# Two buffers of a tuned fp32 kernel start 16 bytes past a multiple of 64

## What is computed

```
h = rms_norm(x); proj = h @ w_in            # retention heads and latent attention, then @ w_out
x = x + conv_ffn(rms_norm(x), w_up, conv_w, conv_b, w_down)
... second block, twice:
  y = mixer(modulate(x)) ; x = layer_norm(alpha*x + g1*y)
  f = peer(modulate(x))  ; x = layer_norm(alpha*x + g2*f)

peer:  s = top-k of query @ keys             # 16 experts for each of 8 heads and each token
       act  = gelu(sum_d h * u_tab[idx])
       out  = sum_k (gate * act) * v_tab[idx]
```

## Time and profile before

| | |
|---|---|
| median of three runs | 2287.6 us (2285.16 to 2290.14) |
| profiled execution | 2285.66 us, of which the span from the first to the last instruction is 2284.3 us |
| mean granted TensorE clock | 0.993 of full speed |
| busy: PE, PEld, DVE, ACT, POOL | 98%, 83%, 82%, 53%, 7% of the span |
| moved by DMA | 442 MB, 194 GB/s over the span |

### The profile page before, as it was taken

The page is one execution under the profiler, slowest core; times in us unless marked ns, Lnnn a source line. Parts: engine busy times, 40 slices in busy tenths (PEclk is TensorE's granted clock), DMA queues, the critical chain, the costliest instruction groups (busy, mean ns, idle before and its releaser), DMA issues.

```text
span 2284.3 us, 34778 instructions
## 1 busy us (share of the span) xinstructions
PE 2233.5 (98%) x13446; PEld 1889.3 (83%) x13446; DVE 1864.8 (82%) x3365; ACT 1201.4 (53%) x1754; POOL 168.5 (7%) x75
## 2 busy tenths in 40 slices
PE   9999999999999999999999999999999999999997
PEld 7789978777788888888887877788888888888886
DVE  8679996568689988888888888869998888887656
ACT  7555554466456555554444445455665554444553
POOL 0000000000044400000000000014430000000000
PEclk9999999999999999999999999999999999999999
DMA  8366593233556655555558996455655555556664
GB/s 292 125 203 217 196 355 117 93 120 102 184 176 185 191 177 170 172 174 175 171 176 306 340 352 233 148 185 186 189 187 169 175 172 171 175 175 223 219 234 136
DMA packets 123508, 442.32 MB, mean 194 GB/s; under 512 B 13760, under 2 KB 16832, under 8 KB 122704
## 3 DMA queue, kind: packets, MB, share of 16 engines
q1 hardware_dynamic: 117464, 425.04, 56.3%
q10 hardware_dynamic: 5880, 15.06, 1.9%
HBM read 436.88 MB, written 3.16 MB: 193 GB/s over the span
## 4 chain that ended last, share of the span: by engine, by line
PE 82%; DVE 10%; ACT 3%; DMA 3%; issue 2%; SPq 0%; ACTq 0%; DVEq 0%
PE psum L447 21%; PE psum L457 13%; PE psum L459 13%; PE psum L458 13%; PE psum L451 12%; PE psum L452 3%; PE psum L2863 3%; DVE low L2607 3%; DVE acc L1784 2%; DMA ring<-in_peer_v 2%; DVE cv L2115 1%; ACT spl L1104 1%; ACT cv L1405 1%; PE psum L925 1%; PE psum L2806 1%
## 5 line engine op out<-in xcount | busy, mean ns | idle before, releaser
L2607 DVE TENSOR_TENSOR low<-ring,spl 128x1024 fp32r<-128x1024 f32 x638 | 778.7, 1228 | 259.3 <-ACT spl L1104 258.8
L1104 ACT ACTIVATE spl<-ring 128x1024 fp32r<-128x1024 f32 x702 | 735.2, 1054 | 281.7 <-DMA ring<-in_peer_u 155.3
L447 PE MATMUL psum<-hT,spl 128*128 128x512 f32 x2016 | 520.0, 397 | 2.5 <-ACT yy_abo L1454 1.4
L447 PEld LDWEIGHTS psum<-hT,spl 128*128 128x128 f32 x2016 | 375.5, 189 | 76.7 <-DVE hT L2454 3.6
L457 PE MATMUL psum<-spl,Ws 128*128 128x512 f32 x1024 | 407.1, 398 | 6.9 <-DVE Ws L2645 6.8
L459 PE MATMUL psum<-spl,Ws 128*128 128x512 f32 x1024 | 399.5, 390 | 0.0
L458 PE MATMUL psum<-low,Ws 128*128 128x512 f32 x1024 | 398.4, 389 | 0.0
L451 PEld LDWEIGHTS psum<-hT,low 128*128 128x128 f32 x2304 | 315.7, 191 | 22.6
L451 PE MATMUL psum<-hT,low 128*128 128x256 f32 x2304 | 322.5, 283 | 0.0
L1713 ACT ACTIVATE Ws<-S 128x256 fp32r<-128x256 f32 x256 | 106.6, 417 | 354.5 <-PE psum L459 349.8
L2920 POOL TENSOR_TENSOR low<-ring,spl 128x1024 fp32r<-128x1024 f32 x64 | 162.1, 2534 | 1133.5 <-ACT spl L1104 1133.5
(11 more groups left out here) (411 smaller groups left out, 2900.1 us busy)
## 6 DMA issues: line engine op xcount, KB each, us to landing
ring<-in_peer_u SPq DMA_DIRECT2D x256, 512.0 KB, 3.5
ring<-in_peer_v SPq DMA_DIRECT2D x256, 512.0 KB, 3.6
vring<-in_ada_w SPq DMA_DIRECT2D x56, 512.0 KB, 6.1
ring<-in_w_up SPq DMA_DIRECT2D x44, 512.0 KB, 5.0
aring<-in_ada_w SPq DMA_DIRECT2D x40, 512.0 KB, 4.9
ring<-in_ab_in SPq DMA_DIRECT2D x32, 512.0 KB, 3.5
ring<-in_peer_wq SPq DMA_DIRECT2D x32, 512.0 KB, 3.8
ring<-in_w_down SPq DMA_DIRECT2D x22, 512.0 KB, 5.9
```

The costliest lines, as they stand in the source:

```text
L447: q.matmul(wide, w(hi, k), P.hT[:, :, k, :], start=k == 0, stop=False)
L1104: q.activation(P.spl[:, m % SLOTS, 0:w], P.ring[:, m % SLOTS, 0:w], ACT.Copy).then_inc(*P.hi.mark(m))
L2607: q.tensor_tensor(P.low[:, n % SLOTS, 0:w], P.ring[:, n % SLOTS, 0:w], P.spl[:, n % SLOTS, 0:w].bitcast(F32), ALU.subtract).then_inc(*P.lo ...
```

## The change

The buffers `ring` and `spl` are allocated 32 words (128 bytes) longer, and their five tiles are taken from word 4 on, so that each tile starts 16 bytes past a multiple of 64. `low` keeps the address of `ring`. All buffers behind the two move up: `spl` by 128 + 16 bytes, everything from `hT` on by 256 bytes, which leaves them as they were modulo 64 and modulo 256. Tile shapes, instructions, waits and their order stay the same.

```diff
         low = self.base + 4 * self.at_word
-        self.ring = f("ring", [128, SLOTS, 1024])
-        self.low = nc.alloc_sbuf_tensor_at("low", [128, SLOTS, 1024], F32R, offset=low)
-        self.spl = f("spl", [128, SLOTS, 1024], F32R)
+        tiles = lambda t: t[:, 4:4 + SLOTS * 1024].rearrange("p (s w) -> p s w", s=SLOTS)
+        self.ring = tiles(f("ring", [128, SLOTS * 1024 + 32]))
+        self.low = tiles(nc.alloc_sbuf_tensor_at("low", [128, SLOTS * 1024 + 32], F32R, offset=low))
+        self.spl = tiles(f("spl", [128, SLOTS * 1024 + 32], F32R))
         self.hT = f("hT", [128, 2, 8, 256], F32R)
```

## The result

The changed kernel took 2296.94 us (median of six runs, 2295.19 to 2301.47) beside 2287.45 us of the kernel before (six runs, 2285.16 to 2290.58): a ratio of 1.0044, 95% interval 1.0033 to 1.0054, or 9.5 us. Forecast were 2287.5 us and a range up to 2300 with "same" as likeliest; by the bound of 0.2% it is slower. The change to the time is clear of the noise, and the forecast of its direction was wrong.

A forecast was written before the change was run, and what follows sets the result against it. PE's matmuls without gaps, 82% of the chain, were taken to bound the kernel. The profiled 2285.7 us plus 0 for PE, VectorE and ScalarE, and DMA gave 2287.5 us as a median, range 2281 to 2300.

The forecast's parts named there:

- What bounds the kernel: Whole chain: PE carries 82% of it, a row of matmuls without holes, with loads, ScalarE and VectorE passes beside it.
- PE's operands at no cost: PE's weight loads and streams of shifted tiles: 0 us added, upper end 27 or 44 us.
- the last sentence of the prediction: Memory handled in units where 32 bytes past is even and 16 is not would make the prediction wrong; rows can't exclude it.
- Buffers that move, at no cost: Buffers behind `ring` and `spl`: they move by 256 bytes, keep their remainder by 64 and 256, and cost nothing.
- VectorE, ScalarE, DMA at no cost: Passes and ring loads on shifted tiles: 0 us each; bounds 0 to 1 us for VectorE, 0 to 20 us for DMA.
- The second rival: Ring loads written in parts: 2288 to 2308 us if only ends cost (6%), 2385 us at half speed (5%).
- the upper part of the range that I had drawn from `rmask`: Ring loads: up to 16% more per KB, 0 to 20 us in two full DMA stretches; the range's high end is 2300.
- The first rival: PE's matmuls streaming a shifted tile each pay 6 ns once: 2314 us, or 2331 us at 10 ns; chance 6%.
- The third rival: Another start lessens collisions between the engines' reads of SBUF: faster by 9 us, 2279 us; chance 5%.
- the 0.07 us behind the scatter: `peer_u` chain: seven matmuls take 1.68 us behind the scatter, 1.61 without; collision if the third rival holds, more likely pipeline refilling.

The follow-up runs named there:

- c2: Every SBUF buffer 32 bytes later than in the kernel before, all distances kept: 2287.7 us, ratio 1.0002.
- b4: Every SBUF buffer 16 bytes later than in the kernel before, all distances kept: 2297.7 us, ratio 1.0040.
- d3: Kernel before with only `Ws` moved, by 64 bytes modulo 256 (and `Eb` behind it to make room): 2298.9 us, ratio 1.0050.
- b1: Kernel before with `ring`, `low` and `spl` in place and all buffers behind them moved up by 256 bytes: 2288.9 us, ratio 0.9999.
- a1: Changed kernel's longer buffers, but their tiles taken from word 0, at a multiple of 64: 2294.0 us, ratio 1.0030 to the kernel before.
- c3: Kernel before with only `hT` 64 bytes later against all others modulo 256: 2281.8 us, ratio 0.9978.
- c1: Every SBUF buffer 64 bytes later than in the kernel before, all distances kept: 2288.1 us, ratio 1.0003.

## Why the prediction was wrong

**What bounds the kernel.** Right, and it made the change matter: PE's row of matmuls has no holes, so a few ns on each reach the time nearly in full (a sum of +9.6 us over the distances for 9.5 us measured).

**PE's operands at no cost.** This is the step that failed. I took 0 from the earlier trace rows, where operands 32 bytes past behave like aligned ones. The row is true, and c2 repeats it for the whole kernel: 32 bytes are free. The step from there to 16 bytes was the error, and the last sentence of the prediction had named it as the one that the rows can't exclude. b4 prices it for all buffers together: 9.6 us, about 4 ns on each matmul of `peer_v`. The weight load's duration, on which I rested the 0, was the wrong row to look at: it doesn't move in d3 either (188 ns), while the distance between matmuls does.

**Buffers that move, at no cost.** I looked at how much each buffer behind moved, by 256 bytes, and that was right (b1: 0.9999). I didn't look at the 128 bytes by which `spl` moved against both `low` and the rest. By a1 this alone is 6.1 us, where the whole change is 9.5. No term of the sum and no rival had it. The two causes don't add up (6.1 and 9.6 against 9.5), so no share of the 9.5 us can be given to either.

**VectorE, ScalarE, DMA at no cost.** Right: 1227 and 1053 ns, a DMA share of 0.88 and 0.89 in the full stretches. (That the queue's share fell from 56.3% to 54.3% is no sign either way: b1, as fast as the kernel before and with its starts modulo 256, has 54.4%.) The second rival (a DMA that pays for its ends) is out, and with it the upper part of the range that I had drawn from `rmask` in the earlier trace rows: its 49 ns per KB is no more than the ring's own queue takes over the whole span, 175 ns for 3.6 KB or 48 ns per KB, with its starts at multiples of 64. The 42 ns per KB that I compared it with was the figure of one short stretch.

**The first rival**, PE pays once per stream, had the right engine and was forecast at 2314 us. Its price, 6 ns on 4,450 streams carried over from VectorE's rows, was too high, and its form was wrong. In the changed kernel the mean distances within a product of `peer_v` go by +6, -2 and 0 ns, +3.6 ns where the shifted tile is the weights of a matmul of 512 columns, and -0.8 ns with 256 columns. I had given it 6%.

**The third rival**, faster by fewer collisions, was 5% and is not what this change did. But c3 shows that another start can be faster, 0.9978 by one buffer 64 bytes farther; that collisions between engines are the reason isn't shown. Its place was not the 0.07 us behind the scatter (1.60 and 1.70 us there, for 1.61 and 1.68 before), but the matmuls of 256 columns. Those 0.07 us come from the first distance behind the scatter, 318 ns; the other five are 227 ns, the shortest of that line. So what I held more likely, a cost of starting anew, fits the trace.

**Two rules beside the runs.** The Trainium skill's page "Collectives: The Full Stack" asks for buffers aligned to 32 bytes ("Rules for kernel authors"). Its number agrees with what b4 and c2 show, but its reason, that this prevents a read-modify-write, isn't what shows here: the loads are no slower (54.3% of 16 engines' span for 56.3%), and the time is in matmuls that only read the buffers. The Trainium skill's page "SBUF — State Buffer", section "Who interferes with whom", calls PE's two read ports, one for the moving operand and one for the weights, independent. The run with only `Ws` moved speaks against it: where the weights stand changes how fast the moving operand's matmuls follow each other, 226.7 or 233.3 ns. The same section says that PE never waits on anyone. As to VectorE and ScalarE the trace agrees (234.0 ns with both busy, 234.2 with both idle).

**What stays open.** That the weight load and the matmul's own read collide is what I make of it, and it isn't shown: both are under way at once, only their addresses change, the pattern of distances repeats from tile to tile, and it doesn't change with what ScalarE and VectorE do. Which of them waits, and on what part of the memory, no run shows. Nor is there a rule from which a time can be worked out ahead: the five places of `hT` give none, and the distances also depend on what ran before them in the stage (227.0 and 233.1 ns for the same places of `hT` and `spl`). That each layout's time is its own, and not chance, rests on b1, c1 and c2, which gave the time of before with other addresses.

## What to carry to other kernels

Where PE runs without holes, start its operands at multiples of 32 bytes, and treat the distances modulo 256 between what it streams and what it loads as weights as something to be tried, on the whole kernel and not by a formula: here 64 bytes were worth -5 us in one place and +12 us in another. When a layout is tested, run the pads alone as well, since the padding may be the larger part of the effect. And read the distance between the starts of matmuls: their durations, and above all those of the weight loads, hide a few ns.

## What the runs showed that I had not expected

- Between layouts that differ by 16 to 128 bytes in the places of a few buffers, the same instructions take 2282 to 2312 us, ratios of 0.9978 to 1.0102.
- With `hT` and `spl` at the same places modulo 256, the matmuls that read them follow each other in 227.0 or 233.1 ns, by where `low` starts.
- Everything 16 bytes later costs 9.6 us; everything 32 or 64 bytes later, 0.6 and 1.0 us, within the noise.
- Matmuls of 256 columns can gain where those of 512 lose: in the run with everything 16 bytes later L460 has 318.2 us for 322.5, and L456 522.3 for 520.0.
- The kernel that came out fastest is the kernel before with `hT` 64 bytes later: 2281.8 us, ratio 0.9978 (0.9968 to 0.9988).
